# Expert prologue: keys and a quarter of the query weights load first, and four folds go ahead of the transposes

## What is computed

```python
h = h + concat([y_ssm, y_diff]) @ w_out          # out projection
m = rmsnorm(h, g_ffn)
# peer(m):
q = (xt @ w_query).reshape(blk, PEER_HEADS, 2, D_KEY // 2)
s = einsum('thcd,cnd->thcn', q, sub_keys)        # scores against 2 x 128 keys, 8 heads
s1, i1 = top_k(s[:, :, 0], 16); s2, i2 = top_k(s[:, :, 1], 16)
# top 16 of the 256 sums per head -> idx, g = softmax; then
u = expert_u[idx]; act = gelu(einsum('thkd,td->thk', u, xt))
out = einsum('thk,thkd->td', g * act, expert_v[idx])
```

## Time and profile before

| | us |
|---|---|
| runs (three) | 3609.58, 3606.58, 3607.18; median 3607.18 |
| profiled execution, span | 3606.9 |
| TensorE busy | 2236.7 (62%) |
| DVE busy | 2216.6 (61%) |
| ACT busy | 1178.5 (33%) |
| POOL busy | 1268.5 (35%) |
| DMA, mean | 349 GB/s |

### The profile page before, as it was taken

How to read it: one execution, slowest core, us unless ns; L and a number is a source line. 1 busy time by engine, 2 the same in 40 slices (tenths; PEclk the granted TensorE clock), 3 DMA queues, 4 the chain that set the end, 5 groups by cost and what they waited for, 6 DMA issues and landing times.

```text
span 3606.9 us, 33674 instructions
## 1 busy us (share of the span) xinstructions
PE 2236.7 (62%) x9892; PEld 765.4 (21%) x9892; DVE 2216.6 (61%) x5337; ACT 1178.5 (33%) x3713; POOL 1268.5 (35%) x1243
## 2 busy tenths in 40 slices
PE   8999967868564554456355545634563654457775
PEld 3556533434110110011011101100110110012222
DVE  5325344626988558656855875586578557855555
ACT  2122214413423322422242242224223321354444
POOL 0000013202544444444444444444444443444342
PEclk9899978989675765567566757756675766577787
DMA  2211148875999999999999999999999999999997
GB/s 101 72 51 62 54 141 320 319 265 214 411 421 421 421 421 419 411 422 420 410 411 421 414 416 416 422 415 407 421 420 413 414 419 416 407 402 415 404 416 327
DMA packets 216450, 1260.05 MB, mean 349 GB/s; under 512 B 28677, under 2 KB 31450, under 8 KB 80882
## 3 DMA queue, kind: packets, MB, share of 16 engines
q0 software_dynamic: 165008, 1147.82, 77.6%
q1 hardware_dynamic: 46106, 101.76, 7.9%
q10 hardware_dynamic: 5152, 8.32, 0.7%
HBM read 1238.27 MB, written 24.05 MB: 350 GB/s over the span
## 4 chain that ended last, share of the span: by engine, by line
DMA 39%; PE 15%; DVE 8%; issue 7%; ACT 6%; POOL 3%; ACTq 0%; POOLq 0%; DVEq 0%; SPq 0%
DMA ex_ring<-in_expert_uv,ex_idx_cur 37%; PE ex_acc L2704 6%; PE ex_pk L2270 4%; POOL ex_ring L2526 3%; DVE ex_ring L2644 3%; PE ex_pk L1783 2%; ACT ex_diag L2582 2%; ACT ex_coef L2576 2%; DMA ex_ring<-in_expert_uv,ex_idx_few 1%; DVE ex_work L1927 1%; PE ex_pk L2138 1%; ACT ex_act_out L2573 1%; PE ex_pt L1753 1%; DVE ex_work L1920 1%; DVE ex_side_f L1932 1%
## 5 line engine op out<-in xcount | busy, mean ns | idle before, releaser
L2644 DVE CUSTOM_DVE_ANT_0 ex_ring<-ex_ring,ex_rows 128x1024 f32<-128x1024 f32 x1056 | 1291.1, 1224 | 849.6 <-DMA ex_ring<-in_expert_uv,ex_idx_cur 814.9
L2526 POOL DMA_INDIRECT ex_ring<-in_expert_uv,ex_idx_cur x1024 | 1136.1, 1109 | 1593.0 <-PE ex_acc L2704 1351.9
L2704 PE MATMUL ex_acc<-ex_ring,ex_diag 128*32 128x512 f32 x4096 | 828.0, 896 | 1107.8 <-ACT ex_diag L2582 1107.5
L2573 ACT ACTIVATE ex_act_out<-ex_dots 128x2 f32<-128x2 f32 x528 | 107.3, 203 | 1703.7 <-DVE ex_dots L2644 1703.1
L2704 PEld LDWEIGHTS ex_acc<-ex_ring,ex_diag 128*32 128x32 f32 x4096 | 97.0, 128 | 1771.5 <-ACT ex_diag L2582 1721.4
L2582 ACT ACTIVATE ex_diag<-ex_pick_row,ex_coef 128x32 f32<-128x32 f32 x1056 | 282.0, 314 | 50.5 <-ACT ex_coef L2576 1.5
L1783 PE MATMUL ex_pk<-ex_w,ex_aT 128*128 128x512 f32 x512 | 253.1, 637 | 0.0
L2576 ACT ACTIVATE ex_coef<-ex_act_out,ex_gate_cur 128x1 f32<-128x1 f32 x1024 | 245.6, 287 | 16.8
L340 PE MATMUL pj_bank<-pj_aT,pj_wbuf 128*128 128x512 f32 x512 | 226.7, 598 | 5.1 <-DVE pj_aT L529 5.1
L2270 PE MATMUL ex_pk<-ex_w,ex_aT 128*128 128x512 f32 x256 | 136.6, 680 | 26.4 <-issue 26.4
L1753 PE MATMUL ex_pt<-ex_wo,ex_aT 128*128 128x512 f32 x256 | 128.9, 647 | 9.1 <-DMA ex_wo<-in_w_out 9.1
(11 more groups left out here) (422 smaller groups left out, 2495.6 us busy)
## 6 DMA issues: line engine op xcount, KB each, us to landing
at_ring<-in_cache_kT SPq DMA_DIRECT2D x64, 256.0 KB, 9.4
at_ring<-in_cache_kT POOLq DMA_DIRECT2D x64, 256.0 KB, 6.0
at_ring<-in_cache_v SPq DMA_DIRECT2D x64, 256.0 KB, 8.9
at_ring<-in_cache_v POOLq DMA_DIRECT2D x64, 256.0 KB, 6.2
ex_ring<-in_expert_uv,ex_idx_cur POOLq DMA_INDIRECT x1024, 13.4
pj_wbuf<-in_w_in SPq DMA_DIRECT2D x6, 2048.0 KB, 10.5
ex_ring<-in_w_queryT SPq DMA_DIRECT2D x4, 2048.0 KB, 15.5
pj_aT<-in_xT_all SPq DMA_DIRECT2D x4, 1024.0 KB, 11.9
```

Of the source, the lines that this page charges most:

```text
L2526: pool.indirect_dma_start(ring[:, c % RING, :], None, t["expert_uv"], bass.IndirectOffsetOnAxis((idx_cur[k % 2] if k < LAST else idx_few)[ ...
L2573: act.activation(act_out[:, half, :], dots[:, half, :], ACT.Gelu).then_inc(gelu_done, 1)
L2644: dve.tensor_tensor_reduce(out=u, in0=u, in1=rows[:, j, :], scale=1.0, scalar=0.0, op0=ALU.mult, op1=ALU.add, accum_out=dots[:, q % HALVES ...
L2704: mm = pe.matmul(acc[n][quarter(j), :], diag[:, q % HALVES, p, :], ring[:, c % RING, D + n * 512:D + (n + 1) * 512], start=False, stop=las ...
```

## The change

Loads: SP issues the keys and the first quarter of the query weights ahead of all else, and no longer holds that quarter back for `w_out`. The other quarters are issued as before. TensorE: folds 0 to 3 stand ahead of the first transposes of `m`; the wait for the copy of fold 3 (`fold_out(pe, 3)`) stands ahead of the first transposes of the few rows; fold 1 waits for nothing but its weights. ACT copies folds 0 and 2 ahead of its first copy of `aT`. DVE copies folds 1 and 3 ahead of its first copy of `aT`, behind its wait for `g`. No instruction on data is added or left out.

```diff
--- before.py
+++ after.py
@@ -1739,9 +1739,12 @@
                 mm.then_inc(turned, 1)
 
             yield from pause(4)
+            if k == 0:
+                fold_queries(pe, 0, 4)
             pe.wait_ge(x_in, 32 * (k + 1))
             turn()
             if k == 0:
+                fold_out(pe, 3)
                 few_turn(pe, 0)
             yield from pause(8)
             pe.wait_ge(taken_a, 2 * k + 1)
@@ -1758,12 +1761,10 @@
                         yield
             if k == 0:
                 few_project(pe)
-                fold_queries(pe, 0, 4)
             yield from pause(18)
             pe.wait_ge(m_ready, k + 1)
             turn()
             if k == 0:
-                fold_out(pe, 3)
                 few_turn(pe, 1)
             yield from pause(8)
             pe.wait_ge(taken_a, 2 * k + 2)
@@ -2090,9 +2091,7 @@
                     pe.wait_ge(wq_in[c // 4], 16)
                 if c == 0:
                     pe.wait_ge(keys_in, 32)
-                elif c == 1:
-                    pe.wait_ge(few_h1, GRP)
-                else:
+                elif c > 1:
                     fold_out(pe, c - 2)
                 if c == 5:
                     pe.wait_ge(few_taken, 2)
@@ -2470,14 +2469,15 @@
         with nc.Block() as block:
             @block.sync
             def _(sp):
+                for c in range(2):
+                    sp.dma_start(keysT[:, c, :], t["keysT"][:, c, :]).then_inc(keys_in, 16)
+                sp.dma_start(wqT[:, 0:4, :], t["w_queryT"][0:4 * P, :].rearrange("(c p) d -> p c d", p=P)).then_inc(wq_in[0], 16)
                 front_sync(sp, 0)
                 sp.dma_start(m_few, t["mix"][SEQ:SEQ + DEC, :]).then_inc(few_in, 16)
                 sp.dma_start(h1_few, t["x_all"][SEQ:SEQ + DEC, :]).then_inc(few_in, 16)
                 sp.dma_start(g[:], spread(t["g_ffn"])).then_inc(g_in, 16)
-                for c in range(2):
-                    sp.dma_start(keysT[:, c, :], t["keysT"][:, c, :]).then_inc(keys_in, 16)
                 sp.wait_ge(wo_in, 16 * KT)
-                for n in range(4):
+                for n in range(1, 4):
                     src = t["w_queryT"][4 * n * P:4 * (n + 1) * P, :].rearrange("(c p) d -> p c d", p=P)
                     sp.dma_start(wqT[:, 4 * n:4 * n + 4, :], src).then_inc(wq_in[n], 16)
                 sp.dma_start(pick_row[:], t["pick_row"]).then_inc(consts, 16)
@@ -2535,13 +2535,13 @@
                     act.dma_start(wo[:, k, :], t["w_out"][k * P:(k + 1) * P, :]).then_inc(wo_in, 16)
                 act.wait_ge(set_up, 2)
                 first = front_scalar(act, 0)
+                fold_take(act, lambda out, src: act.activation(out, src, ACT.Copy), 0, (0, 2))
                 for _ in range(9):
                     next(first)
                 few_take(act, 0)
                 for _ in range(27):
                     next(first)
                 few_square(act)
-                fold_take(act, lambda out, src: act.activation(out, src, ACT.Copy), 0, (0, 2))
                 for _ in range(7):
                     next(first)
                 few_take(act, 1)
@@ -2608,6 +2608,7 @@
                 dve.tensor_copy(iota[:], iota_i).then_inc(set_up, 1)
                 dve.wait_ge(g_in, 16)
                 dve.wait_ge(set_up, 2)
+                fold_take(dve, dve.tensor_copy, 1, (1, 3))
                 first = front_vector(dve, 0, v)
                 for _ in range(33):
                     next(first)
@@ -2615,7 +2616,6 @@
                 for _ in range(6):
                     next(first)
                 few_norm(dve)
-                fold_take(dve, dve.tensor_copy, 1, (1, 3))
                 for _ in first:
                     pass
                 dve.wait_ge(scored, 1)
```

## The result

The changed kernel took 3616.4 us (median of 20 runs) against 3609.44 for the kernel before (20 runs taken beside them). The ratio is 1.0021, with a 95% interval of 1.0013 to 1.0029: by this ratio 7.6 us longer, 4.7 to 10.5 (the two medians differ by 7.0). The forecast was 3.7 us longer and "the same". The time lies just inside the range that was given, but the change is clear of noise, and slower. Both cases of the second rival are out: `w_out` was delayed, and `g` was last. `g` did hold fold 3, as the forecast's mechanism has it, but it came later than forecast, the clock fell in the wait for it (the first rival), and it fell a second time, ahead of the scores, which nothing in the prediction had.

What follows compares the result with a forecast made beforehand. Bound taken: `w_out`'s landing and TensorE's work from there to the scores, shifting all the rest. Projection ends 8.3 us later, minus 4.6 gained behind it, is 3.7: 3607.2 + 3.7 = 3610.9 us, "the same"; range 3605 to 3616.5.

Steps and rivals of the forecast that it cites:

- second rival: Prologue loads: `w_out` not delayed and `g` early, 3601.1 us (chance 0.03); or only `g` early, 3605.4 us (0.12).
- the forecast's mechanism: Before the out projection: fold 3 awaits DVE's fold 1 copy, behind its wait for `g`; projection starts 9.8 us later.
- the first rival: TensorE idles waiting for `g`, clock falls to half from fold 3 on; 4.0 us more, 3614.9 us; chance 0.18.
- the engines are shared packet by packet: Prologue loads: SP's and ACT's queues take turns; 2.1 MB more delays `w_out` by 5.1 us.
- 13.9 us for a warm projection: Out projection of tile 0: runs at full clock throughout, 13.9 us instead of 15.37.
- 9.25 from its end to the scores: Out projection's end to scores: folds gone, the chain over DVE remains, 9.25 us instead of 13.9, gaining 4.6.
- `g` at 23.1, bounds 788 to 791: Prologue loads: `g` lands at 789.5 us, offset 23.1 from the stage's first load issue, between 788 and 791.
- The row of 266 GB/s at 773: Prologue transfers: a rival with slower loads, 2.1 MB costing 7.9 us, total 3614.4 or more; chance 0.05.
- Fold 3 in 2.06, transposes beside the copy: Between `g` and the out projection: fold 3 with handover takes 2.06 us, transposes of `m` run beside DVE's 1.29 us copy.
- From the scores on the program is unchanged: Scores to first gather and later: every piece keeps its place, so the scores' shift passes on one for one.
- the 3 us that the prediction allowed: First gather to the end: a gap differing from before by more than 3 us would show the prediction wrong.
- The first rival with a late `g`: Wait before fold 3: clock falls to half and `g` lands at 791; priced at 3616.4 us.

Runs made afterwards that it cites:

- `h1_few` late: Changed kernel with the `h1_few` load (32 rows, 0.13 MB) issued behind the wait for `w_out`; one run, 3622.1 us.
- The kernel with both gaps filled: Changed kernel plus five unused matmuls in the wait for `g` and three behind the few rows' projection; ratio to before 1.0015.
- one-queue kernels: Changed kernel, `g` awaited late, prologue loads on SP's queue in order of need: 0.9998; with few rows' work also behind the scores: 0.9984.

## Why the prediction was right and wrong

**Right.** That the engines are shared packet by packet, so that both queues end together (`g` at 25.2, `w_out` at 25.4) and `g` instead of `w_out` ends the wait; that DVE's wait for `g` now holds fold 3, and with it transposes and projection; 13.9 us for a warm projection (13.97); 9.25 from its end to the scores (9.30). The sign was right: the first gather came later.

**Wrong, by the terms of the sum** (3.7 forecast, 9.4 measured at the first gather):

- *`g` at 23.1, bounds 788 to 791.* It came at 25.2, beyond the upper bound by 0.6: +2.1. The windows give three parts of some 0.7 each. The 2.1 MB were priced at 410 GB/s, but the transfers' end moved by 5.8 us, not 5.1: the mean of 366, which was taken as the far end, was the right price. The wait ended 1.4 us behind the stop of the full stream instead of 0.7. And `g` was put 0.7 ahead of the last transfer, of which little was left. The row of 266 GB/s at 773 was read as a mischance with a chance of 0.05, though it belongs to the loads of 32 rows. Both kernels have those, so they account for 0.2 or 0.3 of the 2.1, not for all of it.
- *Fold 3 in 2.06, transposes beside the copy.* 3.82 to DVE's copy, then the transposes came last instead of DVE: +2.0 from `g` to the projection. This is the first rival, to which I gave 0.18 because the pause would be shorter than the one at 752 to 757. That row shows that the clock had fallen some 5 us after a stop, not that a shorter pause is safe. The forecast's own pause, from 787 to 790.85, was 3.9 us, and in the kernel with `h1_few` late a pause of 3.7 was enough. So the step that failed is the reading of the row. The late `g` made the pause 4.9; with `g` as forecast and the folds' measured end (21.6) it would have been 2.8, a length that no run here shows.
- *"From the scores on the program is unchanged", each piece keeps its place.* The scores took 8.53 instead of 7.07: +1.5. I counted the 8.2 us of folds between projection and scores as removed work, and missed that they were also what kept TensorE's clock up while DVE did the norm. No rival had this. The kernel with both gaps filled shows it: 7.11. And behind the first gather, the rest of 2759.4 against 2762.5 is past the 3 us that the prediction allowed; its cause is open.
- 3.7 + 2.1 + 2.0 + 1.5 = 9.3. The measured total, 7.6 (4.7 to 10.5), agrees with the prologue's 9.4.

**Luck.** The first rival with a late `g` was priced at 3616.4 us, which is the measured median to the decimal. The terms don't match: of its 4.0 us, fold 3's +1.8 came true, but the projection did not start at half clock (+1.5 that never came) and the transposes cost +0.3, not +0.65. The later `g` and the scores made up for it. The price also stood on a median before of 3607.2, where the runs taken beside the changed kernel give 3609.4. That the time lies inside the range is owed to this.

The Trainium skill's description named under the first rival ("TensorE: Matmul & The Clock Gate", "HAM oscillation — how this bites in real kernels") agrees with the wait for `g`, by the granted clock there and by the kernels that filled it. Two things differ here: the second gap was a wait for DVE's norm, not for a transfer, and the waits for `w_out` of 1.4 and 1.9 us in the one-queue kernels did not take the clock down.

## What to carry to other kernels

Moving a load to the head of one queue delayed the last load of the other queue too (2.1 MB on SP's queue, `w_out` on ACT's 6.2 us later). Before doing so, find the last load that anybody waits for, and put the waits in each engine's program no earlier than their first use (moving one `wait_ge` on `g` was worth 7.6 us here). Work taken off TensorE from between two dependent steps leaves a gap, and the gaps of 3.3 to 4.9 us in this prologue were each followed by a stretch at half clock; count that beside the work saved. And where one long stop is the only row on a risk, it doesn't show that a shorter stop is safe.

## What the runs showed of the hardware

- Loads into 32 partitions: taking 0.13 MB out made what stood behind it land 1.0 to 1.3 us sooner (one profile against four), and both queues ran slowly while such loads passed (315 instead of 416 GB/s).
- The granted clock fell after TensorE had stopped for 4.9 us (changed kernel), 3.7 (`h1_few` late) and 3.3 (before the scores), and held over waits of 1.4 and 1.9 for `w_out` in the one-queue kernels.
- The same projection after the same wait took 15.4 and 16.3 us in two profiles of the kernel before: the granted clock rose 2.8 us behind its start in the one (at 788.0) and 4.7 in the other (at 795.8).
